# ScalarE's order inside a slot: the copy of turned probabilities before probs and exps, side copies first

## The reference

```python
h = rms_norm(x, g_norm1) * (1.0 + scale1) + shift1          # 1024 channels
qa, ka, va, qb, kb, vb, qi, ki, wi, fl, ga, gb = split(h @ w_in)
# mixer B: softmax(q k / 8 + F_q - F_k, causal) @ v          8 heads of 64
# mixer A: index scores pick 128 keys per query, then
#          softmax(q k / 8 - slope * distance, picked) @ v   8 heads of 64
merged = sigmoid(ga) * (oa @ w_o_a) + sigmoid(gb) * (ob @ w_o_b)
x = x + gate1 * (merged @ w_out)
x = x + gate2 * (square(relu(h2 @ w_up)) @ w_down)
```

## Time and profile before

| | |
|---|---|
| Time, median of 3 runs | 993.28 us (993.21 to 996.12) |
| Time of the profiled execution | 994.64 us |
| Its span, first to last instruction | 992.9 us |
| Granted TensorE clock, mean | 0.981 |
| TensorE busy | 944.4 us (95%) |
| VectorE busy | 497.6 us (50%) |
| ScalarE busy | 391.0 us (39%) |
| GpSimd busy | 139.5 us (14%) |
| `probs`, L1455 | 64 times, mean 563 ns, 70.7 us of idle time before them |
| Chain of the work that ended last | TensorE 66%, no wait seen 20%, VectorE 9%, ScalarE 3% |

### The profile page before, as it was taken

One profiled execution on the slowest core, in us unless ns is written; L12 is line 12 of the kernel. 1 busy time (PEld: TensorE's weight loads), 2 busy tenths in 40 slices (PEclk: granted clock), 3 DMA queues, 4 the chain that ended last, 5 costly groups with the idle time before them and its releaser, 6 DMA issues.

```text
span 992.9 us, 19815 instructions
## 1 busy us (share of the span) xinstructions
PE 944.4 (95%) x7546; PEld 862.0 (87%) x7546; DVE 497.6 (50%) x1154; ACT 391.0 (39%) x813; POOL 139.5 (14%) x139
## 2 busy tenths in 40 slices
PE   8889989889899989899999999999999999999998
PEld 7588667767688768798799998999999999999997
DVE  3454767845625678861147556544332244443232
ACT  3254545555556646433333323433311233441121
POOL 4100232141334564310000000000000000000000
PEclk9889999999999989999999999999999999999999
DMA  9536764253422564587423331333223323322312
GB/s 322 186 107 194 185 226 129 96 160 124 132 65 73 167 207 131 158 256 252 143 65 95 98 86 43 85 87 103 86 86 102 87 85 90 100 85 88 103 43 86
DMA packets 176233, 124.54 MB, mean 125 GB/s; under 512 B 14739, under 2 KB 152019, under 8 KB 176164
## 3 DMA queue, kind: packets, MB, share of 16 engines
q1 hardware_dynamic: 176034, 123.50, 40.9%
q10 hardware_dynamic: 130, 0.10, 0.0%
HBM read 116.99 MB, written 6.59 MB: 124 GB/s over the span
## 4 chain that ended last, share of the span: by engine, by line
PE 66%; issue 20%; DVE 9%; ACT 3%; POOL 1%; POOLq 0%; ACTq 0%; DVEq 0%
PE bank L949 18%; PE bank L950 17%; PE bank L951 17%; PE bank L1030 2%; PE bank L1053 2%; PE bank L856 2%; PE bank L1039 2%; PE bank L1009 1%; PE bank L1071 1%; DVE sel L1878 1%; PE bank L878 1%; PE bank L1015 1%; PE bank L1094 1%; PE bank L1084 1%; DVE lg L1905 1%
## 5 line engine op out<-in xcount | busy, mean ns | idle before, releaser
L949 PE MATMUL bank<-h_hi,w_hi 128*128 128x260 f32 x1360 | 397.5, 292 | 8.0 <-DVE h_lo L1762 6.0
L950 PE MATMUL bank<-h_lo,w_hi 128*128 128x260 f32 x1360 | 388.5, 286 | 0.0
L951 PE MATMUL bank<-h_hi,w_lo 128*128 128x260 f32 x1360 | 388.1, 285 | 0.0
L949 PEld LDWEIGHTS bank<-h_hi,w_hi 128*128 128x128 f32 x1360 | 260.1, 191 | 31.6 <-issue 24.0
L951 PEld LDWEIGHTS bank<-h_hi,w_lo 128*128 128x128 f32 x1360 | 260.5, 192 | 0.0
L950 PEld LDWEIGHTS bank<-h_lo,w_hi 128*128 128x128 f32 x1360 | 260.2, 191 | 0.0
L949 PE MATMUL bank<-u_hi,w_hi 128*128 128x260 f32 x512 | 145.2, 284 | 0.0
L950 PE MATMUL bank<-u_lo,w_hi 128*128 128x260 f32 x512 | 144.8, 283 | 0.0
L951 PE MATMUL bank<-u_hi,w_lo 128*128 128x260 f32 x512 | 144.8, 283 | 0.0
L2213 DVE TENSOR_TENSOR w_lo<-raw,w_hi 128x1024 fp32r<-128x1024 f32 x62 | 76.0, 1226 | 135.2 <-ACT w_hi L1638 135.2
L1638 ACT ACTIVATE w_hi<-raw 128x1024 fp32r<-128x1024 f32 x62 | 65.4, 1055 | 140.3 <-PE bank L951 140.3
(11 more groups left out here) (316 smaller groups left out, 1180.9 us busy)
## 6 DMA issues: line engine op xcount, KB each, us to landing
raw<-in_w_in SPq DMA_DIRECT2D x44, 512.0 KB, 4.0
part<-in_w_ada SPq DMA_DIRECT2D x32, 512.0 KB, 5.4
raw<-in_w_up SPq DMA_DIRECT2D x32, 512.0 KB, 4.1
raw<-in_w_down SPq DMA_DIRECT2D x32, 512.0 KB, 4.1
ada<-in_w_ada SPq DMA_DIRECT2D x4, 2048.0 KB, 13.7
kv<-in_cache_k_b SPq DMA_DIRECT2D x16, 256.0 KB, 4.3
qbc<-q_d SPq DMA_DIRECT2D x16, 256.0 KB, 4.5
kv<-in_cache_k_a SPq DMA_DIRECT2D x16, 256.0 KB, 4.2
```

What stands on the lines that cost most here:

```text
L949: mm(out, hi[:, k, :], x_h, start=first and k == ks[0], stop=False)
L950: mm(out, hi[:, k, :], x_l, start=False, stop=False)
L951: end = mm(out, lo[:, k, :], x_h, start=False, stop=last and k == ks[-1])
```

## The change

In ScalarE's list of each slot three things change place. `probs(U-1)` was the first thing of the slot and now stands behind weight rounding, the projection's copy, squares and the conditioning's row. `store_pt(U-2)` stood behind `exps(U)` and now stands ahead of `probs(U-1)`. `exps(U)` comes last of the three. With `probs` gone from the head, `side_store` is the first thing of a slot. The lists of the other engines and all semaphores are as before.

```diff
             for p, s in ITERATIONS:
                 U = SLOTS * (p - 1) + s
                 before = slot_before(p, s)
-                if 0 <= U - 1 < N_UNITS:
-                    probs(U - 1)
                 if before in SIDE:
                     side_store(SIDE.index(before))
                 for i in split_at(p, s):
                     round_w(i)
...
                 if p == 0:
                     for n in range(3 * s, 3 * s + 3):
                         relu_scores(n)
+                if 0 <= U - 2 < N_UNITS:
+                    store_pt(U - 2)
+                if 0 <= U - 1 < N_UNITS:
+                    probs(U - 1)
                 if 0 <= U < N_UNITS:
                     exps(U)
-                if 0 <= U - 2 < N_UNITS:
-                    store_pt(U - 2)
                 if s == 3 and p >= 2:
                     round_o(p - 2)
```

## The result

| | before | after |
|---|---|---|
| Median of 4 runs | 993.25 us (993.12 to 996.12) | 981.39 us (979.9 to 983.25) |
| Profiled execution, its span | 994.64, 992.9 | 980.21, 978.4 |
| Granted clock, mean | 0.981 | 0.980 |

The ratio is 0.9872, 95% interval 0.9853 to 0.9892. Timed again later beside the kernel before, the same kernel had 982.4 us and a ratio of 0.9883 (0.986 to 0.9905). Forecast were 980.6 us and a range of 973 to 989.

What follows compares the result with a forecast made beforehand. A ring of short waits in the slots, no single engine, bounds the kernel. 11.8 us gained plus 2.6 clock minus 1.7 collision made 12.7; 994.64 less 12.7 and 1.36 gave 980.6 us, range 973 to 989.

Steps and rivals of the forecast that it cites:

- exps last: Exps waits for turning, copy and probs in each slot: taken to cost 0 us, bounds 0 and 62.7.
- (a): Copy moved ahead of exps: all 19 TensorE waits at L1039, 17.5 us, go; pair 7 worth 2.2 us, pair 8 2.0.
- (a), slots 5 and 7: Copy's waits in pairs 1 to 6: slot 5 worth 0, in pair 5 0.2 us; slot 7 worth all, 3.2 us.
- (a), the change of pairs: Copy's waits of 1.27 and 2.59 us at changes of pairs: worth 3.4 us, with 0.5 of waiting left.
- (d), the collision: GpSimd's earlier subtractions slow VectorE at fdiag and the last selection steps: 0.7 and 1.0, a loss of 1.7 us.
- (e), the clock: TensorE's lost clock in 200 to 240 and 342 to 378 us: 1.2 and 1.4 come back, bounds 0 and 6.8.
- (b): Probs behind store, side and weight work: outside pair 7, TensorE's wait for mod_row in pair 1 shrinks, worth 0.6 us.
- rival that VectorE takes it back: Pairs 1, 2, 7, 8: removed waits reappear at normalize, o_lo and reciprocal; gain only 5.2, 988.1 us; chance 0.20.

Runs made afterwards that it cites:

- GpSimd held: Kernel after, with GpSimd's subtraction in the first slot of pairs 2 and 3 waiting for the reciprocal behind fdiag: 976.13 us, ratio 0.9819.
- VectorE's order on the kernel before: Kernel before, with the low part of the output ahead of slot 4's logits and normalize ahead of logits in slots 3 and 5: 996.69 us, ratio 1.0016.

## Why the prediction was right

The time was right, by less than a us, and so was the mechanism in the main: the copy's wait went, ScalarE's wait at probs fell from 70.4 to 25.7, and exps last is free (the reciprocal waits 8.1 for L1449, under the 10 of the forecast; before it was 5.7). That the miss is under a us is luck: the stages are off by up to 5 us, both ways. Besides the clock, three of the signs did not come: TensorE's wait at L1084 went up by 2.0 and not by some 4, that at L1039 for L1455 is 4.4 in all and not under 3, and of the fdiags of pairs 2 and 3 only the first got longer; at the second change it was the selection step. The terms:

- *(a), slots 5 and 7.* Right. In pair 1 the 0.68 of slot 5 is gone and TensorE stands 1.91 instead of 1.07 for the normalized keys. From pair 2 on another value takes its place first, the low part of the output (0.84 in slot 5 of pairs 2 to 4, 0.58 in 5 and 6), which the prediction named only for pair 7; the effect is the same. Pairs 4 to 6 gave 2.5 for the 2.1, and the copy alone gives 2.1 there.
- *(a), the change of pairs.* The step that failed is its remainder, "half a us of waiting stays": 1.02 and 2.83 stay. It took probs' end from VectorE's old pace, and VectorE's work was stretched.
- *(d), the collision.* Mis-sized: "0.7 and 1.0" measured 2.08 and 2.07 on VectorE, and 3.8 on TensorE. The assumption that "a part is spent beside GpSimd already under way" fails: a VectorE instruction of this kind that starts inside GpSimd's gets nowhere until that is over (L1884 begins 0.38 behind it and ends 0.29 after it), so it loses nearly all that is left of the 2.4 us. The Trainium skill (GPSIMD Engine Reference, Specifications) names, beside instructions with two SBUF inputs, those of VectorE in a 2-port performance mode. The trace fits the second kind: L1884 reads one tile, takes 0.43 us for 128x512 where a product of two takes 0.69, and is held like fdiag; that it ran in such a mode no trace shows. The prediction had weighed only the first kind.
- *(d), the other way round.* Not foreseen: earlier subtractions also leave places. L1965, 2.87 us on pair 8's path, is 1.03, and pair 8 gave 4.3 for 2.2. That this one instruction is the reason is read from the trace; it was not tried alone, and it can't be all of it: with probs alone it takes 0.83 us, and pair 8 gives only 2.5.
- *(e), the clock.* Mis-sized: the 2.6 measured nothing in the first profile (0.09 x 36 = 3.2 back in 342 to 378, 1.2 lost in 200 to 240, 1.7 in 118 to 160, 0.4 in 160 to 200) and 1.6 in the second (the same 3.2 back, 0.04 x 40 = 1.6 lost in 200 to 240, none in the others). With 2.83 us left at the change it fell there as before, with 0.76 (GpSimd held) it did not. One fall of the kernel before, at 231.5, has no wait over 0.8 us just ahead of it, so that the falls follow the longest waits holds for two of its three. The forecast of over 0.95 in 200 to 240 was wrong for after (0.88) and holds for that experiment (0.96).
- *(b).* The 0.6 itself measured 0.5 (TensorE's waits at L1015 fell from 1.7 to 1.2). But the long waits stood under (a), at the copy, and alone probs behind the head work gives 7.7 us and the copy 2.2. In pair 7 what blocked was probs, and the copy was only the last thing behind it.

The rival that VectorE takes it back had the right engine: 9.7 us of waiting, where 17.5 had gone, came back for values that hang on VectorE. It had the wrong sum, 5.2 us of gain for 11.9: it gave pairs 7 and 8 nothing, and they gave 8.6 to 9.0.

## What to carry to other kernels

In a ring of in-order engines the wait that a profile shows can name the last instruction of a queue and not the one that blocked the queue (pair 7: the copy was named, probs stood in its way): look for what that queue stood for. Moving an instruction earlier moves what it releases on other engines, so list the engine pairs that hold each other up and see what each new place runs beside, and what each old place is freed from. A fix that is worth nothing or costs (VectorE's order on the kernel before, ratio 1.0016) can be worth 5 to 6 us once other bounds are gone (ScalarE's new order and GpSimd held), so try such moves again after each change.

## What the runs showed of the hardware

One GpSimd subtraction of 128x1024 (2.4 us alone) holds back some VectorE instructions that start inside it until it is over, whatever their length: a 0.43 became 2.50, the second half of fdiag with its 0.69 made 3.50 of 1.42, a 0.69 became 2.75. They end 0.29 us after GpSimd's end when they take 0.43 alone, 0.55 after when 0.69, 1.08 after when 1.22 (L2018 of after, at 406.14): about their own length less 0.14. So the price is what is left of GpSimd's instruction, less 0.14. If VectorE's instruction is already running, it is not held (fdiag 1.42 with GpSimd starting 0.79 into it, 0.07 into its second half).

Not every kind is held. The kernel after, slot 4 of pair 7:

```profile
355.11 2.39 POOL L812 TENSOR_TENSOR w_lo<-raw,w_hi 128x1024 fp32r<-128x1024 f32 x1
355.78 0.68 DVE L1918 TENSOR_REDUCE ms<-sq 128x8 f32<-128x512 f32 x1
356.50 1.03 DVE L1919 TENSOR_SCALAR ms<-ms 128x8 f32<-128x8 f32 x1
```

The sum at 355.78 keeps the 0.68 that it has everywhere; the tiny scaling behind it, 0.17 elsewhere, takes 1.03. Held in these traces are operations on two tiles in SBUF, and scalings of one (128x512, 128x8, 8x8; but not 128x1, which keeps its 0.15); sums, maxima, reciprocals, and instructions that read one of their inputs from a bank of TensorE keep their times (L1928 inside a product of GpSimd: 0.69 as elsewhere).

The two places where VectorE was held cost TensorE 3.8 us at the waits, and the pair behind took 2.8 us less with them freed, at a granted clock of 0.96 instead of 0.87. Executions of one kernel differ in their clock: behind the same wait of 1.9 us it fell in one profile of after and not in the other.
